# Expert weight chunks cut by depth over both experts of a pair, and their slots given back at half of each product

## What is computed

```python
def hier_moe(h, grp_w, grp_b, rtr_w, rtr_b, w_gate, w_up, w_down):
    ...
    combine = jnp.sum(jax.nn.one_hot(expert_id, N_EXPERTS, dtype=jnp.float32) * top_w[..., None], axis=1)
    hidden = jax.nn.silu(jnp.einsum('nd,edf->nef', x, w_gate)) * jnp.einsum('nd,edf->nef', x, w_up)
    y = jnp.einsum('nef,efd->nd', hidden * combine[:, :, None].astype(hidden.dtype), w_down)
```

## Time and profile before

| | |
|---|---|
| time before, median of 3 runs | 1363.14 us (1362.69 to 1367.03) |
| the profiled execution's own time | 1359.36 us |
| its span in the trace | 1357.6 us |
| granted TensorE clock, mean | 0.981 of 2.4 GHz |
| busy: PE, DVE, ACT, POOL | 92%, 38%, 22%, 10% of the span |
| DMA queue that carries the weights (q1) | 315.36 MB, 57.5% of 16 engines |
| expert products of layer 0 | first gate product at 322.67 us, overflow passes behind pairs 6 and 7 |
| expert products of layer 1 | first gate product at 1107.91 us, last down product from 1336.58 us |

### The profile page before, as it was taken

The page is one execution under the profiler, slowest core; times in us unless marked ns, Lnnn a source line. Parts: engine busy times, 40 slices in busy tenths (PEclk is TensorE's granted clock), DMA queues, the critical chain, the costliest instruction groups (busy, mean ns, idle before and its releaser), DMA issues. The chain is left out here.

```text
span 1357.6 us, 14639 instructions
## 1 busy us (share of the span) xinstructions
PE 1254.6 (92%) x5786; PEld 704.8 (52%) x5786; DVE 517.5 (38%) x1016; ACT 298.7 (22%) x712; POOL 131.5 (10%) x139
## 2 busy tenths in 40 slices
PE   4999989998999899798999999999999979999897
PEld 2543346445544435244767766776776445454332
DVE  1275666143100002445544645645565551000035
ACT  2123245032111110105121222211232231111112
POOL 0069900000000001001101000000000000000010
PEclk9999999999999999899999999999999999999999
DMA  9859996465999995631232321332234759999994
GB/s 380 331 183 366 372 422 244 168 259 191 383 401 427 425 426 219 283 125 39 102 124 70 140 78 70 132 120 82 78 140 195 316 202 361 411 420 426 425 423 197
DMA packets 35388, 344.67 MB, mean 254 GB/s; under 512 B 3920, under 2 KB 9296, under 8 KB 16080
## 3 DMA queue, kind: packets, MB, share of 16 engines
q1 hardware_dynamic: 23184, 315.36, 57.5%
q0 software_dynamic: 4608, 16.78, 3.1%
q10 hardware_dynamic: 7488, 11.01, 2.2%
HBM read 324.53 MB, written 18.61 MB: 253 GB/s over the span
## 5 line engine op out<-in xcount | busy, mean ns | idle before, releaser
L803 PE MATMUL PS<-ring,hT 128*64 128x512 f32 x736 | 234.8, 616 | 18.8 <-issue 13.8
L610 PE MATMUL PS<-ring,hT 128*128 128x512 f32 x432 | 190.3, 594 | 0.2 <-ACT hT L1150 0.2
L803 PE MATMUL PS<-area,hT 128*64 128x512 f32 x272 | 127.8, 627 | 12.4 <-issue 12.4
L803 PEld LDWEIGHTS PS<-ring,hT 128*64 128x64 f32 x736 | 78.7, 142 | 104.6 <-issue 104.6
L610 PEld LDWEIGHTS PS<-ring,hT 128*128 128x128 f32 x432 | 81.1, 190 | 98.6 <-issue 97.8
L815 PE MATMUL PS<-ring,area 128*64 128x512 f32 x400 | 113.3, 595 | 2.9 <-issue 2.0
L995 PE MATMUL PS<-ring 128*128 128x256 f32 x480 | 108.7, 379 | 1.2 <-ACT ring L1433 1.2
L995 PEld LDWEIGHTS PS<-ring 128*128 128x128 f32 x480 | 91.1, 190 | 13.9 <-issue 1.6
L1973 DVE TENSOR_TENSOR area<-area,PS 128x512 f32<-128x512 f32 x16 | 11.0, 687 | 225.8 <-PE PS L803 225.8
L976 PE MATMUL PS<-ring,area 128*128 128x512 f32 x192 | 83.8, 593 | 3.8 <-ACT area L1521 3.8
L995 PE MATMUL PS<-ring,hT 128*128 128x256 f32 x360 | 82.6, 379 | 0.0
(11 more groups left out here) (302 smaller groups left out, 1506.0 us busy)
## 6 DMA issues: line engine op xcount, KB each, us to landing
ring<-moe_w_down SPq DMA_DIRECT2D x25, 2048.0 KB, 19.3
ring<-mod_w SPq DMA_DIRECT2D x24, 2048.0 KB, 11.6
ring<-moe_w_up SPq DMA_DIRECT2D x24, 2048.0 KB, 15.0
ring<-moe_w_gate SPq DMA_DIRECT2D x22, 2048.0 KB, 15.0
ring<-in_w SPq DMA_DIRECT2D x21, 2048.0 KB, 8.2
area<-moe_w_up SPq DMA_DIRECT2D x8, 2048.0 KB, 13.2
area<-moe_w_gate SPq DMA_DIRECT2D x8, 2048.0 KB, 14.9
ring<-out_w SPq DMA_DIRECT2D x7, 2048.0 KB, 8.1
```

The source lines that it names most:

```text
L610: mm = pe.matmul(out, lhs(k), rhs(k), start=n == 0, stop=n == KD - 1)
L803: mm = pe.matmul(PS[64 * e:64 * e + 64, j, :], g[:, k, 64 * e:64 * e + 64], W[e][k], start=k == 0, stop=k == KD - 1)
```

## The change

The host cuts the experts' weights by depth: chunk 6p holds depth blocks 0 to 3 of the gate matrix for both experts of pair p, chunk 6p+1 blocks 4 to 7; the same for up; for down two blocks each. A chunk still has 2 MB, the order of the stream and the slots are the same. `up` waits for each half's chunk just ahead of its 8 matmuls, and for that half of the gathered tokens. `down` runs both output halves over the first two depth blocks, then both over the last two. Three new semaphores count at half of each product, and `expert_free` counts twice a pair: at the half and at the end. A pair with overflow still gives both halves back from `unit`.

```diff
-                eng.wait_ge(expert_free[c % 6 // 2], PAIRS * l + c // 6 + 1)
+                eng.wait_ge(expert_free[c % 6 // 2], 2 * (PAIRS * l + c // 6) + c % 2 + 1)
...
-                    w = wslot(i)
-                    return [w[:, k, :] for k in range(4 if c % 6 >= 4 else KD)]
+                    w, n = wslot(i), 2 if c % 6 >= 4 else 4
+                    return [[w[:, n * e + k, :] for k in range(n)] for e in range(2)]
...
+                def up(j, p, half_mm):
+                    W = [[], []]
+                    for half in range(2):
+                        w = here(6 * p + 2 * j + half)
+                        if j == 0:
+                            pe.wait_ge(gath_copied, 2 * (base + p) + half + 1)
+                        for k in range(4):
+                            for e in range(2):
+                                mm = pe.matmul(PS[64 * e:64 * e + 64, j, :], gT[:, 4 * half + k, 64 * e:64 * e + 64],
+                                               w[e][k], start=half == 0 and k == 0, stop=half == 1 and k == 3)
+                        if half == 0:
+                            mm.then_inc(half_mm, 1)
+                        W = [W[e] + w[e] for e in range(2)]
+                    return mm, W
...
+                def down(p):
+                    W = [[], []]
+                    for part in range(2):
+                        w = here(6 * p + 4 + part)
+                        for half in range(2):
+                            for k in range(2):
+                                for e in range(2):
+                                    mm = pe.matmul(PS[64 * e:64 * e + 64, 5 + half, :], hidT[:, 2 * part + k, 64 * e:64 * e + 64],
+                                                   w[e][k][:, half * 512:half * 512 + 512],
+                                                   start=part == 0 and k == 0, stop=part == 1 and k == 1)
+                            if part == 1:
+                                mm.then_inc(down_mm, 1)
+                        if part == 0:
+                            mm.then_inc(down_half, 1)
+                        W = [W[e] + w[e] for e in range(2)]
+                    return W
...
-                    pe.wait_ge(gath_copied, 2 * g + 2)
...
-                    act.wait_ge(egate_mm, g + 1)
-                    act.activation(sgate, PS[:, 0, :], ACT.Silu).then_inc(silu_done, 1)
                     with act.If(n < CAP + 1):
+                        act.wait_ge(gate_half, g + 1)
                         act.sem_inc(expert_free[0], 1)
+                        act.wait_ge(egate_mm, g + 1)
+                        act.sem_inc(expert_free[0], 1)
+                        act.activation(sgate, PS[:, 0, :], ACT.Silu).then_inc(silu_done, 1)
+                        act.wait_ge(up_half, g + 1)
+                        act.sem_inc(expert_free[1], 1)
                         act.wait_ge(eup_mm, g + 1)
                         act.sem_inc(expert_free[1], 1)
...
                     with dve.Else():
+                        dve.wait_ge(down_half, g + 1)
+                        dve.sem_inc(expert_free[2], 1)
                         dve.wait_ge(down_mm, 2 * g + 2)
                         dve.sem_inc(expert_free[2], 1)
```

More of the change, by code:

```diff
@@ L769, in here @@
                     if PLACE[i] == APART:
-                        return [v.rearrange("p a b -> p (a b)")[:, 512 * k:512 * k + 512] for v in (gate_row, G) for k in range(4)]
-                    w = wslot(i)
-                    return [w[:, k, :] for k in range(4 if c % 6 >= 4 else KD)]
+                        return [[v.rearrange("p a b -> p (a b)")[:, 512 * k:512 * k + 512] for k in range(4)] for v in (gate_row, G)]
+                    w, n = wslot(i), 2 if c % 6 >= 4 else 4
+                    return [[w[:, n * e + k, :] for k in range(n)] for e in range(2)]
                 def token_rows(p):
@@ L894, in pair @@
                     d = 2 * l + p - DIRECT
-                    pe.wait_ge(gath_copied, 2 * g + 2)
                     if p == 2:
                         pe.wait_ge(gate_copied, 4 * s + 4)
[L898 to L901, removed]
+                    mm, W = up(0, p, gate_half)
+                    mm.then_inc(egate_mm, 1)
+                    mm, w = up(1, p, up_half)
+                    mm.then_inc(eup_mm, 1)
+                    W += w
                     next_tokens(p, 0)
@@ L919, in pair @@
                         gate_rows(s, (0, 1, 2, 3), [1])
-                    W += [here(6 * p + 4), here(6 * p + 5)]
                     pe.wait_ge(hidT_copied, g + 1)
@@ L923, in pair @@
                     need(pe, ov_act, b)
-                    for half in range(2):
-                        down(half, W[4:6]).then_inc(down_mm, 1)
+                    W += down(p)
                     if direct:
@@ L1308, in unit @@
                     with act.If(n < bound):
-                        act.sem_inc(expert_free[0], 1)
+                        act.sem_inc(expert_free[0], 2)
                         act.wait_ge(ov_pe, a + 3)
-                        act.sem_inc(expert_free[1], 1)
+                        act.sem_inc(expert_free[1], 2)
                     act.wait_ge(ov_pe, a + 4)
@@ L1341, in pair @@
                             scale_back(t)
-                    act.wait_ge(egate_mm, g + 1)
-                    act.activation(sgate, PS[:, 0, :], ACT.Silu).then_inc(silu_done, 1)
                     with act.If(n < CAP + 1):
+                        act.wait_ge(gate_half, g + 1)
                         act.sem_inc(expert_free[0], 1)
+                        act.wait_ge(egate_mm, g + 1)
[3 more added lines that the diff above has]
+                        act.sem_inc(expert_free[1], 1)
                         act.wait_ge(eup_mm, g + 1)
                         act.sem_inc(expert_free[1], 1)
+                    with act.Else():
+                        act.wait_ge(egate_mm, g + 1)
+                        act.activation(sgate, PS[:, 0, :], ACT.Silu).then_inc(silu_done, 1)
                     if p + 1 < PAIRS:
@@ L1395, in pair @@
                                 act.nop()
-                        act.sem_inc(expert_free[2], 1)
+                        act.sem_inc(expert_free[2], 2)
                     with act.Else():
@@ L2301, in slots, with pair_halves @@
         return w.reshape(n * r, P, rows // P * columns)
+    def pair_halves(w, k, columns):
+        w = w.reshape(PAIRS, 2, 2, k, P, columns).transpose(0, 2, 4, 1, 3, 5)
+        return w.reshape(2 * PAIRS, P, 2 * k * columns)
     for n, rows, columns in (("mod_w", 256, 2048), ("in_w", D, 512), ("out_w", 512, D)):
@@ L2305 @@
     for n, rows, columns in (("moe_w_gate", D, FF), ("moe_w_up", D, FF), ("moe_w_down", FF, D)):
-        args.append([given(f"{n}{l}", slots(a[f"{n}{l}"].reshape(-1, columns), rows, columns)) for l in range(2)])
+        args.append([given(f"{n}{l}", pair_halves(a[f"{n}{l}"], rows // (2 * P), columns)) for l in range(2)])
     args += [made("y_out", (NT, D)), made("new_k", (KH, P, HD)), made("new_v", (KH, P, HD)),
```

7 lines of the change are left out of this document (4 added, 3 removed).

## The result

| | before | after |
|---|---|---|
| median of 7 runs each, in us | 1363.14 (1358.75 to 1367.03) | 1354.22 (1348.71 to 1357.05) |
| ratio, with its 95% interval | | 0.9928 (0.9908 to 0.9947) |
| the profiled execution's own time | 1359.36 | 1356.17 |
| its span | 1357.6 | 1354.4 |
| granted TensorE clock, mean | 0.981 | 0.977 |

The change makes the kernel 9.8 us faster (0.72% of 1363.14; the medians alone differ by 8.9). The profiled execution of after had a low mean clock (0.977, where the seven executions have 0.977 to 0.986) and shows only 3.2 us of the gain, so the search has to go by places, not by the total.

What follows compares the result with a forecast made beforehand. The prediction took PE's own chain as the bound, with the DMA engines one short step behind. Its terms, -1.4 - 0.1 + 0.8 + 0.9 = +0.2 us, gave 1363.3 us on the median, range 1358.0 to 1368.0.

Steps and rivals of the forecast that it cites:

- J: Follow-up theory: early slots in first pairs leave little queued at PE's jump over overflow code; jump shortens, clock falls go.
- What bounds the kernel: Expert stages: PE's own chain was the bound, DMA engines one short step behind; smallest layer 0 weight margin 2.4 us.
- Slots given back: Expert weight slots freed at half a product: stream 3 to 5 us ahead per layer, no PE wait removed, 0 us.
- The pause: PE's jump over overflow code behind pair 0: longer with weights already flowing, +0.8 us, ends 0 and 2.3.
- The clock: Clock falls just after the pause behind pair 0: more of them, 1.7 us each, +0.9 us, ends 0 and 3.4.
- Start of the gate product: First gate product of each layer: no more 0.69 us wait for ACT's copy of the second token half, -1.4 us.
- Last pair's down: Last pair's down product in layer 1: only the first of two chunks needed at its start, -0.1 us.
- More waits and counts: Added waits on PE, ACT and DVE and three more counting matmuls in each pair: 0 us.
- one slot for two matmuls: Both matmuls of a depth block reading one slot: still side by side, 0 us; otherwise 24 us for a pair.
- The faster one: Rival: weights do bind in ordinary executions, so an earlier stream removes waits for chunks; 1358.6 us, chance 0.14.
- Late rows in the last pair: Rival, layer 1: earlier weight chunks delay DVE's fetched rows, PE's last transposes start 4.2 us late; 1367.5 us, chance 0.07.
- the last sign of being wrong: Whole kernel: the prediction would be wrong if the time fell by 4 us with the pauses unchanged.

Runs made afterwards that it cites:

- run 3: The changed kernel, but each product waits for both of its chunks before its first matmul; slots still given back at half: 1353.45 us against 1364.27 before.
- run 4: The changed kernel once more, unaltered, for the scatter of the jumps: 1352.23 us against 1364.27 for the kernel before.
- run 5: The changed kernel with slots given back at half in pairs 0 and 1 alone: 1354.65 us against 1362.69 for the kernel before.
- run 1: The changed kernel, but both slots of a product are given back at its end: 1361.60 us against 1364.27 for the kernel before.
- run 2: The kernel before, with the gate product starting on the first half of the gathered tokens as its only change: 1362.23 us against 1364.27.
- run 6: The changed kernel with slots given back at half in pairs 2 to 7 alone: 1358.68 us against 1362.69 for the kernel before.
- run 7: The kernel before, loading only the first half of each expert chunk from chunk 12 on (wrong weights, only time counts): 1329.19 us against 1362.69.
- run 10: The changed kernel, SP holding chunk 17 of each layer until PE stands at its jump behind pair 1: 1351.59 us against 1363.67 before.
- run 11: The changed kernel, SP holding chunk 22 of each layer until PE stands at its jump behind pair 2: 1352.89 us against 1363.67 before.
- run 12: The changed kernel, SP holding both chunk 17 and chunk 22 until PE stands at the jump ahead of each: 1349.67 us against 1363.67 before.

## Why the prediction was wrong

The mean of four profiled executions that give back early in pairs 0 and 1 (after, runs 3, 4, 5), less the mean of four that do not (before, runs 1, 2, 6), by the distance from one gate product to the next:

| stretch | layer 0 | layer 1 | of it, clock |
|---|---|---|---|
| start of pair 0 to 1 | -1.26 | -1.26 | 0, 0 |
| 1 to 2 | -0.96 | -0.96 | -0.05, -0.04 |
| 2 to 3 | -1.66 | -1.22 | -1.65, -1.24 |
| 3 to 7 | +0.43 | +3.75 | +1.23, +3.84 |

The first three rows are J: -7.3 us. The last is falls of the clock behind the later pauses, which are as long as before and are followed by a fall in some executions and not in others. In these profiles it cost 4.2 us. The other 3.0 of the 6.1 us by which the profiles differ in the whole lie ahead of the first gate product (-1.8), behind the start of the last (-1.4) and between the layers (+0.2). The ratios over 6 and more executions give 9.8 both for after and for its repeat. That the later falls became more frequent is chance of these profiles, as far as the mean clock can tell: in all 25 timed executions of the four kernels the mean granted clock was 0.9815 and in 57 of before 0.9798, so the lower clock took 25.1 us and 27.5 us of the time, 2.4 us less (uncertain by 0.9), and not more. It is about what the falls behind pair 1 give back (2.9). J's 7.3 and the 1.4 of the gate product's start make 8.7 of the 9.8 us, whose interval is 7.2 to 12.5.

**What bounds the kernel: right.** PE's own chain does. SP waits as long for slots as before (388.6 and 390.4 us), and the kernel is faster all the same. The margin of 2.4 us was real, and run 3 shows that waiting for both chunks costs nothing.

**Slots given back, priced at 0: the step that failed, together with the pause.** "Nobody on PE waits for it, so I price this at 0" looked only for a wait on a weight. PE's sequencer waits for a DMA of its own, the packet of q8, and that one starts the later the more weights are under way: 3.9 us into the jump behind pair 1 before, 2.6 us after. The stream filled the hole as forecast, and for that it had less left when PE jumped. With the falls of the clock that no longer follow, this was worth 7.3 us in the table above.

**The pause, priced at +0.8: wrong in sign.** The step said that weights "already flow again when PE takes that first jump". It compared the DMA share in the 4 us in front of two starts (0.59 and 1.01) and took the low one for an idle machine. The low share was at the end of the jump. From its beginning on, the windows of before read

```profile
345.40:349.40 4.00, 4.00 (x20) 1.15 (x16) 0.00 (x0) 0.60 (x1) 0.00 (x0) 1.00 0.72 307
...
377.20:381.20 4.00, 4.00 (x20) 1.15 (x16) 0.00 (x0) 0.60 (x1) 0.00 (x0) 1.00 1.01 430
```

and even 345.4 to 349.4 had three quarters of a full load, since the second chunk was under way until 349.3. The branch record of 5.36 us, between 6.31 under full load and 3.34 at the last jump of layer 0, would have said that there was more to win than to lose. The pauses measured -1.26 us in each layer behind pair 0, and -0.96 behind pair 1, which had no term at all: the stream had gained its lead by then.

**The clock, priced at +0.9: wrong in sign with it.** The term followed the pause. Behind pair 1, seven of the eight starts of the four kernels without the early give-back had a fall (pauses of 2.4 to 2.6 us), and none of the eight with it (0.99 to 2.0 us): -1.65 and -1.24 us. The size of one fall (1.7 us) was right.

**Start of the gate product, -1.4: right.** The wait of 0.69 us is gone in both layers, and run 2 gave -1.9 with 1.4 in its interval (and 0). **Last pair's down, -0.1: right in kind**, its start waits 0.69 us for ACT and for no chunk. **More waits and counts, one slot for two matmuls: 0, as measured**: gate and up product take 13.95 us in both profiles. The prediction had this from a misread row: its 33 records "without a count" begin with the last record of the gate product and end with that of the up product, and both count. The Trainium skill, TensorE: Matmul & The Clock Gate, section on the cost of packing, would have made 1.3 us of the counts; the equal 13.95 us show nothing of it.

**The rivals.** The faster one foresaw the sign for a wrong reason: it had weights bind, and run 3 refutes this. Late rows in the last pair did not come: DVE had 3.24 us to spare ahead of the hidden values instead of 0.76. The Trainium skill, Runtime: NRT & Kernel Launch, section on instruction fetch, was cited for the pause, that a jump fetches its target by DMA: the trace agrees, with a 16 KB packet of kind "instruction" inside each of 196 jumps, which starts 1.0 us in where few weights are under way (run 7, pair 1) and 3.9 us in where many are (before, pair 1). Carried to its end it would have put the right question: the fetch is the one transfer that PE did wait for, so what matters is where each one meets the stream. Of the last sign of being wrong, the fall in time by 4 us came, but with the pauses shorter, not unchanged. (The low end of the sum, -1.6, makes 1361.5 and not 1361.6.)

## What to carry to other kernels

Where PE takes a branch between products, read that branch's own record: how long it lasts, how far ahead of the last matmul it starts, and what is queued on the DMA engines from its first moment on. Only what exceeds the sequencer's lead (4 us here) is a pause, so 1 or 2 us off the queue at that moment can be worth more than weights that come earlier, and a transfer held back until the engine stands at its jump shortens that jump although its data comes later (to 3.2 to 4.2 us in runs 10 to 12, from the 5.0 to 6.4 us of after and runs 3 to 5). Look for the packet of kind "instruction" inside the branch record: it says how long the fetch waited. In the waits, "issue" says that the profile names no semaphore; it does not say that nothing was waited for.

## What the runs showed that was not expected

- The same jump took 3.2 to 3.8 us with the DMA engines near idle and 5.7 to 6.6 under a full weight stream (6.9 twice, in runs 2 and 10). Rows of 4 KB instead of 16 KB did not change this, and held the stream to 408 GB/s at a share of 1.02, where before reached 418 at 1.00.
- A fall of the clock lasted 3.4 us. Before, 6 of 11 starts behind pauses of 1.9 to 2.5 us had one; in the profiled executions of after and of runs 3 to 5 none of the 16 starts behind pairs 0 and 1 had one, with pauses of 0 to 2.0 us.
- With half of the weights' bytes from chunk 12 on, the kernel takes 34 us less, though PE had waited 0.8 us for weights.
